# Order and start addresses of the on-chip tensors in a fused two-block transformer kernel with 768 expert gathers

## The reference, cut to what matters

```python
q = (xb @ w_q).reshape(TOK_BLOCK, PEER_HEADS, 2, PEER_DHALF)
s = jnp.einsum('thcd,hcnd->thcn', q, sub_keys).astype(jnp.float32)
top_s, top_i = lax.top_k(s, K)                       # K = 16, 128 keys in each half
cand = top_s[:, :, 0, :, None] + top_s[:, :, 1, None, :]
best_s, best_c = lax.top_k(cand.reshape(TOK_BLOCK, PEER_HEADS, K * K), K)
...
e = (i1 * PEER_NKEYS + i2).reshape(TOK_BLOCK, PEER_HEADS * K)   # 128 experts per token
gate = jax.nn.softmax(best_s, axis=-1).reshape(TOK_BLOCK, PEER_HEADS * K)
u = expert_u[e]
act = jax.nn.gelu(jnp.einsum('td,ted->te', xb, u), approximate=False)
coef = (gate * act.astype(jnp.float32)).astype(xb.dtype)
return jnp.einsum('te,ted->td', coef, expert_v[e])
```

## Time and profile before

| | |
|---|---|
| Median of three runs | 2518.23 us (2517.28 to 2520.91) |
| Profiled execution: its own time | 2512.19 us |
| Profiled execution: span from the first to the last instruction | 2510.4 us |
| TensorE clock granted, mean | 0.982 of full |
| Busy: TensorE, VectorE, ScalarE, GpSimd | 89%, 66%, 36%, 34% |
| Moved by DMA | 942.30 MB, mean 375 GB/s over the span |

### The profile page before, as it was taken

The page is one execution under the profiler, slowest core; times in us unless marked ns, Lnnn a source line. Parts: engine busy times, 40 slices in busy tenths (PEclk is TensorE's granted clock), DMA queues, the critical chain, the costliest instruction groups (busy, mean ns, idle before and its releaser), DMA issues.

```text
span 2510.4 us, 30004 instructions
## 1 busy us (share of the span) xinstructions
PE 2232.6 (89%) x9846; PEld 1277.0 (51%) x9846; DVE 1659.9 (66%) x3971; ACT 913.5 (36%) x2668; POOL 865.9 (34%) x796
## 2 busy tenths in 40 slices
PE   9989989989988889989989988889899989977776
PEld 7877745544454445545545554435555535523222
DVE  3864566666665677666677666667667767777664
ACT  2232233333343434343443334434335533433232
POOL 0012044344333343333334343234333444344442
PEclk9999999999999999999999999999999999999999
DMA  5421589999999999999999999999999999999996
GB/s 195 134 69 36 196 346 421 421 421 421 421 420 421 416 386 421 420 421 421 419 406 421 421 416 421 394 422 416 421 419 406 407 420 421 421 421 420 418 418 279
DMA packets 151656, 942.30 MB, mean 375 GB/s; under 512 B 16864, under 2 KB 19136, under 8 KB 53072
## 3 DMA queue, kind: packets, MB, share of 16 engines
q0 software_dynamic: 110592, 805.36, 77.5%
q1 hardware_dynamic: 40912, 135.05, 14.0%
HBM read 939.29 MB, written 1.05 MB: 375 GB/s over the span
## 4 chain that ended last, share of the span: by engine, by line
PE 41%; DMA 41%; DVE 9%; ACT 5%; issue 3%; POOL 0%; DVEq 0%; ACTq 0%; POOLq 0%
DMA arena<-in_uv,idx 40%; PE bank L1909 24%; PE bank L371 5%; DVE arena L1937 5%; PE bank L1546 2%; ACT arena L1975 1%; PE bank L1558 1%; PE bank L844 1%; PE bank L865 1%; DMA weights<-in_sb_v 1%; PE bank L602 1%; DVE arena L1215 1%; ACT arena L1963 1%; PE bank L831 1%; ACT arena L1969 1%
## 5 line engine op out<-in xcount | busy, mean ns | idle before, releaser
L1909 PE MATMUL bank<-arena 128*128 128x512 f32 x3072 | 1438.4, 613 | 239.9 <-ACT arena L1975 233.0
L1994 POOL DMA_INDIRECT arena<-in_uv,idx x768 | 838.2, 1091 | 1423.1 <-PE bank L1909 1299.0
L1909 PEld LDWEIGHTS bank<-arena 128*128 128x128 f32 x3072 | 569.4, 194 | 946.7 <-issue 594.0
L1937 DVE CUSTOM_DVE_ANT_0 arena<-arena,h 128x1024 f32<-128x1024 f32 x512 | 627.4, 1225 | 399.7 <-DMA arena<-in_uv,idx 395.1
L1963 ACT ACTIVATE arena<-arena 128x2 f32<-128x2 f32 x384 | 78.1, 203 | 1194.1 <-DVE arena L1937 1193.9
L1937 DVE CUSTOM_DVE_ANT_0 arena<-arena 128x1024 f32<-128x1024 f32 x256 | 313.9, 1226 | 215.1 <-DMA arena<-in_uv,idx 213.8
L371 PEld LDWEIGHTS bank<-xT,weights 128*128 128x128 f32 x1808 | 250.6, 191 | 51.9 <-issue 34.9
L371 PE MATMUL bank<-xT,weights 128*128 128x128 f32 (+2 forms) x1808 | 269.3, 304 | 0.0
L1975 ACT ACTIVATE arena<-const,arena 128x128 f32<-128x128 f32 x768 | 260.5, 386 | 0.0
L1969 ACT ACTIVATE arena<-arena 128x1 f32<-128x1 f32 x768 | 184.8, 288 | 12.6
L1963 ACT ACT_TABLE_LOAD x73 | 93.7, 1283 | 1.3
(11 more groups left out here) (333 smaller groups left out, 1850.9 us busy)
## 6 DMA issues: line engine op xcount, KB each, us to landing
weights<-in_w_q SPq DMA_DIRECT2D x42, 512.0 KB, 8.6
weights<-in_w_in SPq DMA_DIRECT2D x38, 512.0 KB, 3.5
weights<-in_a_fm SPq DMA_DIRECT2D x28, 512.0 KB, 9.2
arena<-in_uv,idx POOLq DMA_INDIRECT x768, 13.9
weights<-in_a_out SPq DMA_DIRECT2D x16, 512.0 KB, 8.2
weights<-in_b_fm SPq DMA_DIRECT2D x16, 512.0 KB, 7.8
weights<-in_b_out SPq DMA_DIRECT2D x16, 512.0 KB, 9.8
arena<-in_w_q SPq DMA_DIRECT2D x14, 512.0 KB, 13.2
```

Of the source, the lines that this page charges most:

```text
L1909: ins = nc.tensor.matmul(acc[:, :], diag[:, e % DIAGS, :], ring[:, e % RING, at:at + 512], start=first, stop=last)
L1937: V.tensor_tensor_reduce(out=u, in0=u, in1=x, scale=1.0, scalar=0.0, op0=ALU.mult, op1=ALU.add, accum_out=dots[:, unit % 2, kx:kx + 1]).th ...
L1994: nc.gpsimd.indirect_dma_start(out=ring[:, s, :], out_offset=None, in_=io[f"uv{unit // PH // NT}"], in_offset=bass.IndirectOffsetOnAxis(ap ...
```

## The change

The on-chip tensors are declared in another order: `arena` first, then the other large ones, and the small ones behind them. `arena` also grows by 16 floats per partition, from 38,640 to 38,656. No instruction is added, removed or moved, no shape used by an instruction changes, and the wait on every semaphore is what it was.

```diff
@@ -217,19 +217,19 @@
+        ARENA = 38656
+        arena_t = sbuf("arena", [P, ARENA])
+        weights = sbuf("weights", [P, SLOTS, D])
+        h = sbuf("h", [P, NT, D])
+        rows = sbuf("rows", [P, 2, D])
+        xT = sbuf("xT", [P, KC, TALL])
+        row_parts = sbuf("row_parts", [10 * KC, P])
         const = sbuf("const", [P, NCONST_KEEP])
         cols = sbuf("cols", [P, NCOLS])
-        h = sbuf("h", [P, NT, D])
-        xT = sbuf("xT", [P, KC, TALL])
-        weights = sbuf("weights", [P, SLOTS, D])
-        rows = sbuf("rows", [P, 2, D])
-        row_parts = sbuf("row_parts", [10 * KC, P])
         small = sbuf("small", [P, 64])
         idx_best = sbuf("idx_best", [P, 2, PK], U32)
         idx_pos = sbuf("idx_pos", [P, 3, PK], U32)
         idx = sbuf("idx", [P, 2, PK], U32)
-        ARENA = 38640
-        arena_t = sbuf("arena", [P, ARENA])
```

## The result

The changed kernel takes 2525.36 us in the median of ten runs (2522.36 to 2532.85), the one before 2517.48 us in ten (2514.95 to 2520.91). The ratio is 1.0030 with a 95% interval of [1.0019, 1.0041]: slower by 0.3%, some 8 us. The forecast was no change.

What follows compares the result with a forecast made beforehand. The prediction took the DMA rate as the bound from about 320 us on and TensorE and its feed before 300 us. Changes of 0 + 0 + 0 left the median's scale, 2518 us, with a range of 2510 to 2527.

Steps and rivals of the forecast that it cites:

- no change: Whole kernel: start addresses cost nothing, 2518 us, own range 2512 to 2525; chance 0.90.
- What bounds the kernel: From about 320 us on, bytes divided by the DMA rate; before 300 us, TensorE and what feeds it.
- The addresses: New order puts `arena`, `weights`, `h`, `xT`, `rows` and `row_parts` at 128 past a multiple of 512, not at one.
- The cost of a start address: DMA into on-chip tensors: moving `weights` costs 0 (upper end 1/16 of its time), the ring gains 0 (upper end 0.8%).
- the direct pair of 4 KB stretches: `weights` at 9 to 15 us, 25.5 GB/s, against `w_o` at 265 to 271 us, 25.4: read as one rate.
- that only the gathers pay: Sign of being wrong: the start address, within multiples of 64 bytes, has a price for the gathers alone.
- Case 4: Weight rows touch 17 instead of 16 blocks of 256 bytes: 14.9 us slower, 2533 us; chance 0.03.
- Case 3: Rows pay for bytes below their 256 boundary: ring saves 14.9 us, weights lose 7.4, net 2510 us; chance 0.02.
- Case 5: TensorE reads slower from the new starts ahead of the stream; at 3% 8 us, 2526 us; chance 0.02.
- the engines that read: VectorE's ring product (1225 ns) and TensorE's 128x128 product (275 ns) do not depend on the start: 0 for both.
- Case 2: Ring rows of 8 KB get faster at 128 than at 192: 0.8%, 16 us, 2502 us; chance 0.03.

Runs made afterwards that it cites:

- true512: Changed kernel with a 384-byte gap ahead of `arena`, so all large tensors start at a multiple of 512: 2496.02 us, ratio 0.9911 to the kernel before.
- arena256: Kernel before, same order, only `arena` moved from 448 to 256 past a multiple of 512: 2492.64 us, ratio 0.9914.
- arena128: Kernel before, same order, only `arena` moved from 448 to 128 past a multiple of 512: 2514.00 us, ratio 0.9991.
- rest384: Kernel before with `h`, `xT` at 384 and `rows`, `row_parts` at 128 past a multiple of 512, weight slots at 0, arena at 448: 2517.51 us, ratio 0.9996.

## Why the prediction was wrong, point by point

**What bounds the kernel.** Right, and it is why a change without an instruction shows at all: where the engines move bytes without a pause, a piece that takes 1% longer is time.

**The addresses.** Right. `arena` landed at 128 past a multiple of 512, not at one, and took all large tensors with it. That the change does not make what its name says was the first half of the answer; true512, which does, gains 0.9%.

**The cost of a start address.** This is the step that failed: "I take 0 for both, because the direct pair of 4 KB stretches is the nearest row." It took six microseconds of one load for the price of a start. What the runs showed in its place is a price for starting off a multiple of 256: 0.23 to 0.30% for the slots, 6 to 8 us, and about 1% for the ring.

First, the row is a fair reading of its six microseconds and not of the load. Between 265 and 271 us 10 of the 608 pieces of 4 KB that go to `w_o` take 160 ns or more. From 272 us on, with `w_o` still landing until about 275 us, it is some 70% of them. The same trace in the next window, 271 to 277 us, and then arena256, whose arena starts on a boundary, in the same window:

```profile
q1 hardware_dynamic: 677, 2.48, 102.9%
```

```profile
q1 hardware_dynamic: 689, 2.52, 102.7%
```

That is 25.1 against 25.6 GB/s for a busy engine, and 162.1 ns a piece in the first. So the price stood in the trace of before, ahead of any gather, right behind the stretch that was read; the pair of stretches was equal by luck of the window. How large it is depends on what moves beside it, and nearly nine tenths of the time is spent in another mix, with the gathers: the price had to come from there.

Second, for the ring there was no row at all. The rows compared starts at 192 and at 128 past a multiple of 256, both off a boundary, and gave 26.0 and 26.2 GB/s for a busy engine. No row of 8 KB in the trace started on one, where the value is 26.4. From those two I put the gain of a better ring at 0.8%, for a step from 192 to 128, and gave it 0.03. That step is worth nothing that can be told (arena128, 0.9991), as forecast. The reason given, that "the 4 KB rows of `w_o` start at the same 192 as the ring and pay nothing", is refuted twice: `w_o` does pay, and the ring at 192 pays 1% of the kernel. The prediction named, among its signs of being wrong, a price "that only the gathers pay"; both queues pay it.

**Case 4, the weights get slower (0.03).** This is what happened: the slots lost their multiple of 256 and nothing else mattered. Its size was off by half. It had 6.25% more for each row, 14.9 us; the queue's own pieces became 1.6% dearer (128.1 to 130.1 ns, or 1.5% by the 4 KB pieces alone), the larger part of the loss sits in the ring's pieces beside them (25.92 to 25.81 GB/s), and the medians put both together at 6 to 8 us. That in the stream it is seen only beside a ring off its own boundary was not in it.

**Case 3, the bytes below the boundary are paid for (0.02).** Refuted in its form: it grades by the bytes, and the slots cost the same at 64, 128 and 192 past a boundary (1.0030, 1.0024, 1.0029), while the ring at 64, 128 and 192 shows 0.9997, 0.9991 and 1.
**Case 5 and the engines that read.** Right to leave at nothing: 1225 ns and 275 to 276 ns are the same in both layouts, and rest384, in which `h` and `xT` start at 384, is 0.9996.

**Case 2.** Not in this change, and not for its step: 192 and 128 cost the ring the same. That the ring pays for its start at all is the largest effect found, some 25 us.

The measured median lies in the stated range, since that reached to other cases (its upper part to a TensorE that reads slower); the range did not rest on the mechanism that moved the time. The chance of 0.90 for no change was far too high for a sum that rested on one pair of stretches.

What stays open is why only some of the misplaced pieces take longer, why their share changes between executions of one kernel (35% and 3% in the stretch from 9 to 15 us), and why misplaced slots cost nothing beside a ring on its boundary, where 2% of the 4 KB pieces take 160 ns or more against 49 to 65% beside a misplaced ring. Pieces have a duration in the traces; nothing shows what happens inside one.

## What to carry to other kernels

Where the DMA engines are the wall, work out the absolute byte at which every DMA target starts, reserved bytes at the front included, and put the busiest one at a multiple of 256; here a gap of 16 floats made 25 us of 2517. Padding sizes to a round number does not do it if the base is off. And take a price from a stretch with the same mix of transfers as the one in which it will be paid, and from more than one stretch: the six microseconds read here showed no price, and the ones right behind them did.

## What the runs showed of the hardware that was not expected

- A write into on-chip memory by DMA is dearer when its row starts off a multiple of 256 bytes: 26.0 against 26.4 GB/s for a busy engine with rows of 8 KB; 64, 128 and 192 past it are alike within the intervals of the times, and 512 is no better than 256.
- It is not a fixed extra for each piece. With the ring and the slots on a boundary, 0.2 to 0.3% of the 4 KB pieces in the stream take 160 ns or more; with both off it is 49 to 65%, and the others keep their 159 ns.
- The price of one queue's start depends on the other's: slots off a boundary cost 0.23 to 0.30% beside a ring off its own, and nothing (0.9893 against 0.9910) beside one on it.
- The granted TensorE clock can stand at half speed for part of the first 30 us in one execution (0.66 between 10 and 30 us) and not in the next of the same kernel (1.00), with TensorE busy throughout in both; the first gather came at 323.1 us in the one and at 317.3 in the other. Four of the other seventeen profiles show such a fall too (0.74), in layouts of every kind, with the first gather at 320.3 to 323.7 us.
